# Adding the second gate block's halves on VectorE in the later feature-major chunks

## The chip, the core and the metric

The kernel runs on one core of a Trainium2 chip. The metric is the time of one execution on the device, in microseconds. A core has a matrix engine (TensorE, PE in the rows; its weight loads are listed apart as PEld), VectorE (DVE), ScalarE (ACT), GpSimd (POOL) and SyncE (SP), which issues most of the transfers. Every engine works through its own list of instructions in order, and semaphores tie the lists together.

## The reference

Two layers of a decoder on 256 tokens of width 1024, in float32: each layer has a gated feed-forward (FFN), a mixer and a second FFN, each followed by a layer norm. The change touches the FFN alone:

```python
def swiglu(x, w_in, w_out):
    gate, up = jnp.split(x @ w_in, 2, axis=-1)
    return (jax.nn.silu(gate) * up) @ w_out

x = layer_norm(ALPHA * x + 0.5 * swiglu(x, ffn1_w_in[l], ffn1_w_out[l]), ln_gain[l, 0], ln_bias[l, 0])
```

There are four FFNs, called F0, F1, F2 and F3; the mixers AB and C stand between F0 and F1 and between F2 and F3. The hidden width is 2816.

## The kernel before, in words

Float32 accuracy is made of products of rounded numbers: a weight w is split into w_hi, a rounded copy that ScalarE makes, and w_lo = w - w_hi, which VectorE makes; activations likewise. TensorE multiplies high by high and adds the two mixed products.

An FFN is cut into 11 chunks of 256 hidden features, numbered 0 to 10. For each chunk three units of weights come in from memory through a ring of three raw buffers (`raw`): two with the gate and up columns, and a product block with rows of `w_out`. Chunks 0, 1 and 10 are computed with tokens in the partitions. Chunks 2 to 9 are feature-major: features in the partitions, four blocks of 128 features in a chunk, the first two of the gate, the last two of the up half. A block (`up_block`) is one psum bank of 512 columns: 256 tokens with the high part of x beside the same 256 with its low part, both against w_hi, and the product with w_lo added to the first half. The two halves of 256 columns must still be added, for the gate before the Silu. All four blocks of a chunk use the same bank `G[0]`, so the next block's first matmul waits until ScalarE has copied the one before it out (`up_copy`, semaphore `up_copied`): gate blocks to `GATES` (which lies in `ffn_tok`), up blocks to `UPS`. Between the blocks TensorE has products of the chunk before (lines 2026), five or six matmul passes, to work on.

Who adds the halves: for the up blocks VectorE, both at once, line 1067 (`up_add`). For each gate block GpSimd issues a transfer from SBUF to SBUF that adds on its way, line 1717 (`add_gates`): 64 of them, two for each of the 32 feature-major chunks. ScalarE's Silu of both gate blocks (line 579) waits for both transfers. Then VectorE multiplies (`up_product`, line 1079), forms sums of hidden blocks (`hidden_sums`, lines 1043 to 1048; the down projection is a Strassen-like scheme with seven products) and sums of the next product block's weights (`weight_sums`, lines 1013 to 1019), which ScalarE rounds at line 515 ahead of the second gate block's copy.

The order on each engine is written out by hand. VectorE's list in one feature-major chunk: additions and sums as above, the rest of the hidden blocks (1053, 1059), the splits of the weight sums (1031) and of two gate and up units (995), and the split of the product block's rest (`split_plain_lo`, line 1001), which waits for ScalarE's cast of that block (line 509). Beside that VectorE makes rotary tables in chunks 4, 5 and 6 of F0, and prepares bounds of mixer C in chunk 4 of F1 and chunk 3 of F2 (`beside`). GpSimd's list holds the adding transfers, in F0 with loads of tables between them: a pool's weights behind chunk 4, constants behind chunk 5, and a norm's gain and bias behind chunk 6.

Of the kernel before, what the change touches and what calls it, by code (L numbers as in the profile page):

```python
# [17 lines left out]
ALU = mybir.AluOpType  # L18
# [9 lines left out]
SEQ = 256  # L28
# [7 lines left out]
N_PROD = NC - 2  # L36
N_COPY = 2
FIRST_FM = 2
N_FM = NC - 1 - FIRST_FM
STD_CHUNK = {0: 0, 1: 1, NC - 1: 2}  # L40
N_T = N_COPY + 2
# [34 lines left out]
def build(nc, x, positions, ln_gain, ln_bias, ffn1_w_in, ffn1_w_out, ffn2_w_in, ffn2_w_out, ab_w_in, ab_w_o,  # L76
          diff_lambda, diff_subln, pool_w, pool_scale, c_w_in, c_w_o, c_norm, hgrn_gamma, consts, out):
    with ExitStack() as ctx:
# [3 lines left out]
        def sem(name):  # L82
            return ctx.enter_context(nc.semaphore(name))
# [63 lines left out]
        sums_hi, sums_lo, sums_used = sem("sums_hi"), sem("sums_lo"), sem("sums_used")  # L147
        sums_half = sem("sums_half")
        up_done, up_copied = sem("up_done"), sem("up_copied")
        gate_added = [sem(f"gate_added{j}") for j in range(2)]  # L150
        up_added, x_added = sem("up_added"), [sem(f"x_added{i}") for i in range(4)]
        gate_silu, hid_product = sem("gate_silu"), sem("hid_product")
        early_used, late_hi, late_lo = sem("early_used"), sem("late_hi"), sem("late_lo")
# [55 lines left out]
        SILUS = {"F0": 0, "F1": 1, "F2": 2, "F3": 3}  # L209
# [19 lines left out]
        for m, name in enumerate(ORDER):  # L229
# [3 lines left out]
            for u, kind in enumerate(kinds):  # L233
# [20 lines left out]
                chunk = pairs - (kind == "B")  # L254
                if name in FFN and kind in "AB" and FIRST_FM <= chunk < NC - 1:
                    occupant[slot] = (up_done, 4 * (N_FM * SILUS[name] + chunk - FIRST_FM + 1), 0)
                elif kind in "AO":
# [94 lines left out]
        GATES = ffn_tok[:].rearrange("p a t f -> p (a t f)").rearrange("p (b f) -> p b f", b=2)  # L352
# [125 lines left out]
        def _(act):  # L478
# [88 lines left out]
            def up_copy(name, c, b):  # L567

                f = SILUS[name]
                act.wait_ge(up_done, 4 * (N_FM * f + c - FIRST_FM) + b + 1)  # L570
                if c > FIRST_FM:
                    act.wait_ge(hid_product, N_FM * f + c - FIRST_FM)
                nc.scalar.copy((UPS[name] if b // 2 else GATES)[:, b % 2], G[0]).then_inc(up_copied, 1)  # L573

            def gates_silu(name, c):

                for j in range(2):
                    act.wait_ge(gate_added[j], 16 * (N_FM * SILUS[name] + c - FIRST_FM + 1))
                nc.scalar.activation(GATES[:, :, 0:SEQ], GATES[:, :, 0:SEQ], ACT.Silu).then_inc(gate_silu, 1)

            def ffn(name, m):
# [42 lines left out]
                for c in range(FIRST_FM, NC - 1):  # L624
# [32 lines left out]
                    else:  # L657
# [7 lines left out]
                                     ).then_inc(copied_out, 1)  # L665
                act.wait_ge(hid_product, N_FM * (f + 1))
                act.wait_ge(sums_used, N_PROD * (f + 1))
# [313 lines left out]
        def _(dve):  # L981
# [8 lines left out]
            def split_lo(n):  # L990

                if n >= N_UNITS:
                    return
                dve.wait_ge(hi_ready, nth[n])
                nc.vector.tensor_tensor(w_lo[:, slot_of[n]], raw[:, n % RAW], w_hi[:, slot_of[n]].bitcast(F32),  # L995
                                        ALU.subtract).then_inc(lo_ready, 1)
# [37 lines left out]
            def hidden_sums(name, c):  # L1034
# [6 lines left out]
                else:  # L1041
                    dve.wait_ge(hid_product, N_FM * f + c - FIRST_FM + 1)
                nc.vector.tensor_tensor(s1, a21, a22, ALU.add).then_inc(hid_step1, 1)
# [12 lines left out]
            def hid_late_lo(name, c):  # L1056
# [2 lines left out]
                nc.vector.tensor_tensor(hT_lo_flat[:, LATE], hid_blocks[:, LATE_HID], hT_hi_flat[:, LATE].bitcast(F32),  # L1059
                                        ALU.subtract).then_inc(late_lo, 1)  # L1060

            def up_add(name, c):

                f = SILUS[name]
                ups = UPS[name]
                dve.wait_ge(up_copied, 4 * (N_FM * f + c - FIRST_FM + 1))
                nc.vector.tensor_tensor(ups[:, :, 0:SEQ], ups[:, :, 0:SEQ], ups[:, :, SEQ:], ALU.add
                                        ).then_inc(up_added, 1)
# [88 lines left out]
            def ffn_hidden(name, t, g, nth, hid):  # L1157

                dve.wait_ge(silu_ready, 2 * SILUS[name] * len(STD_CHUNK) + nth + 1)
                nc.vector.tensor_tensor(hid, g[:, FC:2 * FC], ffn_tok[:, 0, t], ALU.mult).then_inc(hid_ready, 1)  # L1160

            def ffn(name, m):
                s0, f = phases[name], SILUS[name]

                if m == 0:
                    ffn_hidden(name, 0, G[0], 0, ffn_tok[:, 1, 0])
                    weight_sums(name, s0 + 4, 0)
                    ffn_hidden(name, 1, G[1], 1, ffn_tok[:, 1, 1])
                    weight_sums(name, s0 + 4, 1)
                    split_lo(s0 + 3)  # L1170
                    split_plain_lo(s0 + 4)
                    hidden_sums(name, 0)
                    split_lo(s0 + 5)
                    hid_early_lo(name, 0)
                    ffn_hidden(name, 0, G[0], 2, ffn_tok[:, 0, 0])
                    ffn_hidden(name, 1, G[1], 3, ffn_tok[:, 0, 1])
                    hid_late_lo(name, 0)
                    split_sums_lo(name, s0 + 4, True)
                else:
                    xT_split(m, 0)  # L1180
                    norm(ORDER[m - 1], 1)
                    ffn_hidden(name, 0, G[0], 0, ffn_tok[:, 1, 0])
                    split_lo(s0 + 3)
                    xT_split(m, 1)
                    weight_sums(name, s0 + 4, 0)
                    weight_sums(name, s0 + 4, 1)
                    ffn_hidden(name, 0, G[1], 1, ffn_tok[:, 0, 0])
                    split_plain_lo(s0 + 4)
                    split_sums_lo(name, s0 + 4)
                    ffn_hidden(name, 1, G[0], 2, ffn_tok[:, 1, 1])  # L1190
                    if name == "F1" and BEFORE_C:
                        layer_c_tables()
                    hidden_sums(name, 0)
                    hid_early_lo(name, 0)
                    hid_late_lo(name, 0)
                    ffn_hidden(name, 1, G[1], 3, ffn_tok[:, 0, 1])
                    split_lo(s0 + 5)
                split_lo(s0 + 6)
                hidden_sums(name, 1)
                split_plain_lo(s0 + 7)  # L1200
                last = NC - 2
                for c in range(FIRST_FM, NC - 1):
                    n = s0 + 3 * c + 1
                    if c > FIRST_FM:
                        up_add(name, c - 1)
                        up_product(name, c - 1)
                        hidden_sums(name, c - 1)
                    weight_sums(name, n, 0)
                    weight_sums(name, n, 1)
                    if c == FIRST_FM + 1:  # L1210
                        split_lo(n + 1)
                        hid_early_lo(name, c - 1)
                    else:
                        hid_early_lo(name, c - 1)
                        split_lo(n + 1)
                    hid_late_lo(name, c - 1)
                    beside(name, c)
                    split_sums_lo(name, n)
                    split_lo(n + 2)
                    if c < last:  # L1220
                        split_plain_lo(n + 3)
                split_lo(n + 3)
                up_add(name, last)
                up_product(name, last)

                n, c = s0 + FFN_UNITS - 1, NC - 1
                dve.wait_ge(hidT_hi, NH * f + c)
                nc.vector.tensor_tensor(hT_lo[:, 0], hid_blocks[:, 0:512], hT_hi[:, 0].bitcast(F32), ALU.subtract
                                        ).then_inc(hidT_lo, 1)
                sums_out(name)  # L1230
                split_lo(n)
                ffn_hidden(name, 0, G[0], 4, ffn_tok[:, 1, 0])
                split_lo(n + 1)
                dve.wait_ge(x_added[0], 16 * (f + 1))
                dve.wait_ge(moved_out, 2 * f + 2)
                x0 = x_tok[:, 0].rearrange("p (h f) -> p h f", h=2)
                step(nc.vector.tensor_tensor(x0, x0, kept_both.unsqueeze(1).to_broadcast([P, 2, 512]), ALU.add))
                last_hidT(name, 0)
                split_lo(n + 2)
                norm_stats(name, 0)  # L1240
                norm_gain(name, 0, (0,))
                ffn_hidden(name, 1, G[1], 5, ffn_tok[:, 1, 1])
                norm_gain(name, 0, (1,))
                last_hidT(name, 1)
                norm_scale(name, 0)
                split_lo(n + 3)
# [443 lines left out]
        def _(pool):  # L1690
# [21 lines left out]

            def add_gates(name, chunks):
                for c in chunks:
                    for j in range(2):
                        pool.wait_ge(up_copied, 4 * (N_FM * SILUS[name] + c - FIRST_FM) + j + 1)
                        pool.dma_start(GATES[:, j, 0:SEQ], GATES[:, j, SEQ:], accum_op=ALU.add).then_inc(gate_added[j], 16)  # L1717

# [796 lines left out]
```

## Time and profile before

| | |
|---|---|
| Median of 3 runs | 965.91 us (965.4 to 967.02) |
| The profiled execution | 964.49 us, of which the profiled span is 962.8 us |
| Busy, TensorE / VectorE / ScalarE / GpSimd | 952.3 / 849.0 / 620.4 / 108.7 us |
| Granted TensorE clock | 0.998 of full |
| Moved by transfers | 197 MB, 205 GB/s in the mean |

The span is the time from the first to the last instruction of the profiled execution; the rest of its time lies around it. A row of the timeline gives start, duration, engine and line, what is written from what, and in brackets how long the engine was idle before it and what ended that. An engine that is busy for nearly all of the span need not be at its peak, since matmuls overlap and their ends are modelled.

### The profile page before, as it was taken

Reading aid. Unit: us, or ns where it says so; the run is one execution under the profiler, and the core shown is the slowest. Engines: PE = TensorE matmul, PEld = TensorE weight load, DVE = VectorE, ACT = ScalarE, POOL = GpSimd, SP = SyncE. Lnnn points to the kernel's source line nnn. Section 1 sums busy time; section 2 is a strip of 40 time slices with the busy share of each in tenths; the row PEclk is TensorE's granted clock in tenths of the full one; section 3 lists DMA queues with packets and bytes.
Section 4 is the critical chain, followed back from the end, with each engine's and each line's share of the span. In section 5 each row is a group of like instructions: output and inputs, shape, how many; then the busy total and the mean of one; then the engine's idle time right before and its main releaser. Section 6 shows DMA issues by size and latency. Waiting matters only on the chain.

```text
span 962.8 us, 13790 instructions
## 1 busy us (share of the span) xinstructions
PE 952.3 (99%) x4904; PEld 806.8 (84%) x4904; DVE 849.0 (88%) x1174; ACT 620.4 (64%) x727; POOL 108.7 (11%) x146
## 2 busy tenths in 40 slices
PE   9999999999999999999999999999999999999996
PEld 7888888888888888888888888888888888888885
DVE  5999998996898999889889989899898997999886
ACT  6776667436646667675576666549998546667660
POOL 0211111100210111110011101100100100111110
PEclk9999999999999999999999999999999999999999
DMA  9778877753656786876587777935243656786761
GB/s 306 240 228 234 280 235 223 232 178 129 223 180 205 217 244 193 236 227 206 173 237 235 239 231 232 271 124 184 89 131 115 235 192 190 215 242 194 237 162 55
DMA packets 140912, 197.31 MB, mean 205 GB/s; under 512 B 7280, under 2 KB 114336, under 8 KB 140720
## 3 DMA queue, kind: packets, MB, share of 16 engines
q1 hardware_dynamic: 126032, 173.56, 55.3%
q0 software_dynamic: 14256, 22.38, 11.1%
q8 instruction: 40, 0.66, 0.3%
q10 hardware_dynamic: 560, 0.52, 0.2%
q14 instruction: 24, 0.20, 0.1%
HBM read 182.79 MB, written 1.06 MB: 191 GB/s over the span
## 4 chain that ended last, share of the span: by engine, by line
PE 91%; DVE 5%; ACT 2%; issue 1%; DMA 1%; POOL 0%; DVEq 0%; SPq 0%; ACTq 0%
PE psum L2012 23%; PE psum L2026 15%; PE psum L2019 12%; PE psum L1821 12%; PE psum L1830 12%; PE psum L1825 12%; DVE w_lo L995 1%; PE psum L2402 1%; ACT w_hi L503 1%; PE psum L1814 1%; PE psum L2388 1%; DVE w_lo L1031 1%; DMA raw<-in_ffn_w_out 1%; DVE w_lo L1001 1%; PE psum L1996 1%
## 5 line engine op out<-in xcount | busy, mean ns | idle before, releaser
L995 DVE TENSOR_TENSOR w_lo<-raw,w_hi 128x2048 fp32r<-128x2048 f32 x125 | 285.1, 2284 | 20.9 <-ACT w_hi L503 20.8
L2012 PE MATMUL psum<-xT,w_hi 128*128 128x512 f32 x1024 | 254.2, 390 | 0.5
L503 ACT CAST w_hi<-raw 128x2048 fp32r<-128x2048 f32 x125 | 238.3, 1914 | 24.5 <-DMA raw<-in_ffn_w_in 15.0
L2012 PEld LDWEIGHTS psum<-xT,w_hi 128*128 128x128 f32 x1024 | 191.3, 188 | 44.8 <-ACT ffn_tok L573 3.2
L2019 PEld LDWEIGHTS psum<-xT,w_lo 128*128 128x128 f32 x1024 | 139.7, 190 | 10.0
L2019 PE MATMUL psum<-xT,w_lo 128*128 128x256 f32 x1024 | 142.8, 282 | 0.0
L1821 PE MATMUL psum<-w_hi,xT 128*128 128x512 f32 x447 | 128.7, 399 | 0.8 <-DVE arena L1538 0.4
L1830 PE MATMUL psum<-w_hi,xT 128*128 128x512 f32 x447 | 124.8, 390 | 0.2 <-DVE xT L1099 0.2
L1825 PE MATMUL psum<-w_lo,xT 128*128 128x512 f32 x447 | 124.7, 390 | 0.0
L1717 POOL DMA_DIRECT2D ffn_tok<-ffn_tok x64 | 55.0, 859 | 484.7 <-ACT ffn_tok L573 484.7
L1830 PEld LDWEIGHTS psum<-w_hi,xT 128*128 128x128 f32 x447 | 83.9, 188 | 18.3 <-DVE xT L1099 0.5
L1825 PEld LDWEIGHTS psum<-w_lo,xT 128*128 128x128 f32 x447 | 83.9, 188 | 17.7
L1821 PEld LDWEIGHTS psum<-w_hi,xT 128*128 128x128 f32 x447 | 80.8, 188 | 16.8 <-DVE ffn_tok L1160 0.8
L573 ACT COPY arena<-psum 128x512 f32<-128x512 f32 x64 | 37.6, 587 | 71.2 <-PE psum L2019 71.1
L1031 DVE TENSOR_TENSOR w_lo<-arena,w_hi 128x2048 fp32r<-128x2048 f32 x35 | 80.0, 2284 | 0.1
L1001 DVE TENSOR_TENSOR w_lo<-raw,w_hi 128x1536 fp32r<-128x1536 f32 x36 | 63.1, 1754 | 15.9 <-ACT w_hi L509 15.9
L573 ACT COPY ffn_tok<-psum 128x512 f32<-128x512 f32 x64 | 37.5, 586 | 59.3 <-PE psum L2019 45.1
L515 ACT CAST w_hi<-arena 128x2048 fp32r<-128x2048 f32 x36 | 68.9, 1915 | 10.5 <-DVE arena L1019 8.9
L2026 PE MATMUL psum<-w_hi,hT_hi 128*128 128x512 f32 x232 | 75.4, 395 | 0.0
L2026 PE MATMUL psum<-w_lo,hT_hi 128*128 128x512 f32 x232 | 75.1, 393 | 0.0
L2026 PE MATMUL psum<-w_hi,hT_lo 128*128 128x512 f32 x232 | 69.8, 393 | 0.0
L509 ACT CAST w_hi<-raw 128x1536 fp32r<-128x1536 f32 x36 | 53.5, 1485 | 14.5 <-PE psum L2026 7.9
(220 smaller groups left out, 1165.3 us busy)
## 6 DMA issues: line engine op xcount, KB each, us to landing
raw<-in_ffn_w_in SPq DMA_DIRECT2D x170, 512.0 KB, 5.2
raw<-in_ffn_w_out SPq DMA_DIRECT2D x88, 512.0 KB, 4.4
raw<-in_c_w_in SPq DMA_DIRECT2D x32, 512.0 KB, 4.7
ffn_tok<-ffn_tok POOLq DMA_DIRECT2D x64, 128.0 KB, 4.9
raw<-in_ab_w_in SPq DMA_DIRECT2D x16, 512.0 KB, 4.9
x_tok<-arena POOLq DMA_DIRECT2D x16, 256.0 KB, 7.3
raw<-in_ab_w_o SPq DMA_DIRECT2D x8, 512.0 KB, 4.2
raw<-in_c_w_o SPq DMA_DIRECT2D x8, 512.0 KB, 4.0
```

Source lines behind the costliest of these rows:

```text
L503: nc.scalar.copy(w_hi[:, slot_of[n]], raw[:, n % RAW]).then_inc(hi_ready, 1)
L515: nc.scalar.copy(w_hi[:, SUMS], SUM_PLACES[name].rearrange("p a f -> p (a f)")).then_inc(sums_hi, 1)
L573: nc.scalar.copy((UPS[name] if b // 2 else GATES)[:, b % 2], G[0]).then_inc(up_copied, 1)
L995: nc.vector.tensor_tensor(w_lo[:, slot_of[n]], raw[:, n % RAW], w_hi[:, slot_of[n]].bitcast(F32), ALU.subtract).then_inc(lo_ready, 1)
L1001: nc.vector.tensor_tensor(w_lo[:, PLAIN, 0:1536], raw[:, n % RAW, 512:], w_hi[:, PLAIN, 0:1536].bitcast(F32), ALU.subtract).then_inc(plain ...
L1031: nc.vector.tensor_tensor(w_lo[:, SUMS], SUM_PLACES[name].rearrange("p a f -> p (a f)"), w_hi[:, SUMS].bitcast(F32), ALU.subtract).then_in ...
L1821: nc.tensor.matmul(dst, a_hi, b_hi, start=first, stop=False)
L1825: ins = nc.tensor.matmul(dst, a_hi, b_lo, start=False, stop=final and last)
L1830: ins = nc.tensor.matmul(dst, a_lo, b_hi, start=False, stop=final and last)
L2012: nc.tensor.matmul(G[0], w_hi[:, slot_of[n + kh], at:at + P], xT_both[:, 4 * kh + k].rearrange("p a s -> p (a s)"), start=kh == k == 0, st ...
L2019: ins = nc.tensor.matmul(G[0][:, 0:SEQ], w_lo[:, slot_of[n + kh], at:at + P], xT_hi[:, 4 * kh + k], start=False, stop=kh == 1 and k == 3)
L2026: return nc.tensor.matmul(PROD[p], a[:, A_OF[p] * P:(A_OF[p] + 1) * P], w[:, slot, part * 512:(part + 1) * 512], start=start, stop=stop)
```

## The change

From the third feature-major chunk on (chunks 4 to 9 of each FFN, 24 of the 32) the halves of the second gate block are added by VectorE (`gate_sum`), placed between the split of the second gate and up unit and the split of the product block's rest; the transfer for it is not issued. The first gate block keeps its transfer, and chunks 2 and 3 keep both. The Silu waits for the new semaphore instead of the second transfer's.

```diff
+N_BY_DMA = 2
...
-        gate_added = [sem(f"gate_added{j}") for j in range(2)]
+        gate_added, gate_summed = [sem(f"gate_added{j}") for j in range(2)], sem("gate_summed")
...
             def gates_silu(name, c):
 
-                for j in range(2):
-                    act.wait_ge(gate_added[j], 16 * (N_FM * SILUS[name] + c - FIRST_FM + 1))
+                f, k = SILUS[name], c - FIRST_FM
+                act.wait_ge(gate_added[0], 16 * (N_FM * f + k + 1))
+                if k < N_BY_DMA:
+                    act.wait_ge(gate_added[1], 16 * (N_BY_DMA * f + k + 1))
+                else:
+                    act.wait_ge(gate_summed, (N_FM - N_BY_DMA) * f + k - N_BY_DMA + 1)
                 nc.scalar.activation(GATES[:, :, 0:SEQ], GATES[:, :, 0:SEQ], ACT.Silu).then_inc(gate_silu, 1)
...
+            def gate_sum(name, c):
+
+                dve.wait_ge(up_copied, 4 * (N_FM * SILUS[name] + c - FIRST_FM) + 2)
+                nc.vector.tensor_tensor(GATES[:, 1, 0:SEQ], GATES[:, 1, 0:SEQ], GATES[:, 1, SEQ:], ALU.add
+                                        ).then_inc(gate_summed, 1)
...
                     split_sums_lo(name, n)
                     split_lo(n + 2)
+                    if c >= FIRST_FM + N_BY_DMA:
+                        gate_sum(name, c)
                     if c < last:
                         split_plain_lo(n + 3)
...
                 for c in chunks:
-                    for j in range(2):
+                    for j in range(2 if c < FIRST_FM + N_BY_DMA else 1):
                         pool.wait_ge(up_copied, 4 * (N_FM * SILUS[name] + c - FIRST_FM) + j + 1)
                         pool.dma_start(GATES[:, j, 0:SEQ], GATES[:, j, SEQ:], accum_op=ALU.add).then_inc(gate_added[j], 16)
```

Line numbers of the changed kernel are higher by 5 on VectorE up to the new function and by 13 behind it. VectorE's list in chunk 4 of F0, from the split of the weight sums (1031) to the sum of the up halves (1067), before:

```order
L1282 TENSOR_SCALAR arena<-arena 128x64
L1283 TENSOR_SCALAR arena<-arena 128x64
L1031 TENSOR_TENSOR w_lo<-arena,w_hi 128x2048
L995 TENSOR_TENSOR w_lo<-raw,w_hi 128x2048
L1001 TENSOR_TENSOR w_lo<-raw,w_hi 128x1536
L1067 TENSOR_TENSOR arena<-arena 128x2x256
```

and in the changed kernel, where line 1070 is the new addition:

```order
L1295 TENSOR_SCALAR arena<-arena 128x64
L1296 TENSOR_SCALAR arena<-arena 128x64
L1036 TENSOR_TENSOR w_lo<-arena,w_hi 128x2048
L1000 TENSOR_TENSOR w_lo<-raw,w_hi 128x2048
L1070 TENSOR_TENSOR ffn_tok<-ffn_tok 128x256
L1006 TENSOR_TENSOR w_lo<-raw,w_hi 128x1536
L1078 TENSOR_TENSOR arena<-arena 128x2x256
```

One instruction has been put in ahead of the product block's rest; the rest of VectorE's order is the same. GpSimd's list in F0 before, from the transfers of chunks 2 to 4 on (ffn_tok is where the gates lie):

```order
L1717 DMA ffn_tok<-ffn_tok 128x256 x6
L1747 DMA arena<-in_pool_w 128x4x128
L1717 DMA ffn_tok<-ffn_tok 128x256 x2
L1749 DMA arena<-shape_constants 128x1536
L1717 DMA ffn_tok<-ffn_tok 128x256 x2
L1705 DMA ln_gb<-in_ln_gain 128x1024
L1705 DMA ln_gb<-in_ln_bias 128x1024
```

and in the changed kernel:

```order
L1730 DMA ffn_tok<-ffn_tok 128x256 x5
L1760 DMA arena<-in_pool_w 128x4x128
L1730 DMA ffn_tok<-ffn_tok 128x256
L1762 DMA arena<-shape_constants 128x1536
L1730 DMA ffn_tok<-ffn_tok 128x256
L1718 DMA ln_gb<-in_ln_gain 128x1024
L1718 DMA ln_gb<-in_ln_bias 128x1024
```

The loads of tables now stand behind the first transfer of chunks 4, 5 and 6, and no longer behind a second one.

## Rows read from the trace of the kernel before

**Rows 1.** The page: busy times of the engines, and the chain's shares.

```profile
PE 952.3 (99%) x4904; PEld 806.8 (84%) x4904; DVE 849.0 (88%) x1174; ACT 620.4 (64%) x727; POOL 108.7 (11%) x146
...
PE 91%; DVE 5%; ACT 2%; issue 1%; DMA 1%; POOL 0%; DVEq 0%; SPq 0%; ACTq 0%
```

**Rows 2.** F0, chunk 7: length, busy time by engine, clock, DMA share, GB/s.

```profile
114.91:130.84 15.93, 15.93 (x87) 13.77 (x86) 14.33 (x15) 11.04 (x12) 1.75 (x2) 1.00 0.86 268
```

**Rows 3.** Waits: who for whom; total us, times, longest.

```profile
DVE w_lo L1001 <- ACT w_hi L509: 15.9, 17, 1.1
...
PEld psum L2012 <- ACT ffn_tok L573: 3.2, 7, 0.6
...
ACT ffn_tok L579 <- DMA ffn_tok<-ffn_tok: 0.3, 1, 0.3
```

**Rows 4.** VectorE's timeline, F0, chunk 7: start, duration, instruction, idle before.

```profile
122.93 0.42 DVE L1059 TENSOR_TENSOR hT_lo<-arena,hT_hi 128x256 fp32r<-128x256 f32 x1
123.27 2.28 DVE L1031 TENSOR_TENSOR w_lo<-arena,w_hi 128x2048 fp32r<-128x2048 f32 x1
...
128.80 1.76 DVE L1001 TENSOR_TENSOR w_lo<-raw,w_hi 128x1536 fp32r<-128x1536 f32 x1 [1.05 <-ACT w_hi L509]
130.84 0.69 DVE L1067 TENSOR_TENSOR arena<-arena 128x512 f32<-128x512 f32 x1 [0.29 <-ACT arena L573]
```

**Rows 5.** VectorE in F1, chunk 4 and chunk 9.

```profile
343.48 1.76 DVE L1001 TENSOR_TENSOR w_lo<-raw,w_hi 128x1536 fp32r<-128x1536 f32 x1 [0.22 <-ACT w_hi L509]
...
423.99 2.29 DVE L995 TENSOR_TENSOR w_lo<-raw,w_hi 128x2048 fp32r<-128x2048 f32 x1 [1.63 <-ACT w_hi L503]
```

**Rows 6.** VectorE in F0: sums in chunks 5 and 6, end of 6.

```profile
88.11 0.69 DVE L1019 TENSOR_TENSOR arena<-raw,arena 128x512 f32<-128x512 f32 x1
...
103.77 0.69 DVE L1019 TENSOR_TENSOR arena<-raw,arena 128x512 f32<-128x512 f32 x1
...
114.91 0.69 DVE L1067 TENSOR_TENSOR arena<-arena 128x512 f32<-128x512 f32 x1 [0.29 <-ACT arena L573]
```

**Rows 7.** ScalarE in F0: copies and casts of chunks 5 to 7.

```profile
90.64 0.58 ACT L573 COPY ffn_tok<-psum 128x512 f32<-128x512 f32 x1
...
95.42 1.48 ACT L509 CAST w_hi<-raw 128x1536 fp32r<-128x1536 f32 x1 [0.40 <-PE psum L2026]
98.36 0.59 ACT L573 COPY arena<-psum 128x512 f32<-128x512 f32 x1 [1.46 <-PE psum L2019]
...
106.44 0.59 ACT L573 COPY ffn_tok<-psum 128x512 f32<-128x512 f32 x1
...
122.37 0.59 ACT L573 COPY ffn_tok<-psum 128x512 f32<-128x512 f32 x1 [0.35 <-PE psum L2019]
```

**Rows 8.** Weight loads in F0: third block of chunks 5 and 6.

```profile
91.28 0.19 PEld L2012 LDWEIGHTS psum<-xT,w_hi 128*128 128x128 f32 x1
...
107.17 0.19 PEld L2012 LDWEIGHTS psum<-xT,w_hi 128*128 128x128 f32 x1
```

**Rows 9.** All 64 adding transfers: time from issue to landing.

```profile
DMA to landing us min/median/max: 2.7/4.9/7.8
```

**Rows 10.** GpSimd's timeline in F0, chunk 5.

```profile
87.23 0.84 POOL L1717 DMA_DIRECT2D ffn_tok<-ffn_tok  x1 [9.95 <-ACT ffn_tok L573]
91.52 0.85 POOL L1717 DMA_DIRECT2D ffn_tok<-ffn_tok  x1 [3.44 <-ACT ffn_tok L573]
92.06 0.88 POOL L1749 DMA_DIRECT2D arena<-shape_constants  x1
```

**Rows 11.** Loads in F0: product block at 88.9, gate units at 91.9, 123.2.

```profile
L422 SPq DMA_DIRECT2D raw<-in_ffn_w_out x2: 346/346/346, 89.0 to 89.5; - x2
...
DMA to landing us min/median/max: 4.1/4.6/5.0
...
DMA to landing us min/median/max: 4.9/6.3/7.7
...
DMA to landing us min/median/max: 4.3/5.1/5.9
```

## The prediction

> **What bounds the kernel now.** Read the page's busy times first, then the chain: TensorE is busy 99% of the span and holds 91% of the chain that ended last [rows 1]. So time is won or lost only where TensorE waits. The stretch table says the same of one feature-major chunk, from one addition of the up halves to the next: 15.93 us, TensorE busy for all of it, VectorE for 14.33, the granted clock 1.00, the 2.4 GHz level [rows 2]. VectorE thus has 1.6 us of room in a chunk. Next the table of waits: the weight loads of the gate and up blocks waited 3.2 us in 7 places for a gate copy out of psum; VectorE waited 15.9 us in 17 places for ScalarE's cast of a product block; and ScalarE's Silu waited for the adding transfers once, for 0.3 us [rows 3]. That last row is all that the transfers cost visibly today.
>
> **What is removed.** Of 32 feature-major chunks 24 lose the transfer of the second gate block. The Silu waited 0.3 us for a transfer once [rows 3]. In its chunk the delay ended inside VectorE's own room, so I count this gain as nothing. The transfers' traffic (24 times 128 KB) lies beside weight loads that ScalarE reads without a wait in the steady chunks; I count that as nothing too.
>
> **What is added, and its price.** VectorE does 24 additions of 128x256 numbers, two operands and the result in SBUF. No row of before has just this one. The nearest is the 128x256 subtraction of line 1059: its own duration is 0.42 us, but the next instruction starts 0.34 us after it (122.93 to 123.27) [rows 4]. What a full VectorE loses is the distance of starts, so I take 0.34 and keep 0.42 as the upper end; the in-place addition of twice the size takes 0.69 [rows 4], so nothing dearer is near. The Trainium skill ("VectorE: DVE Perf Modes", section "The TRN2 errata — SBUF-src ops pay a fixed extra latency per instruction") puts an fp32 add at N plus 151 cycles of 0.96 GHz, which is 0.42 us as an estimate; by it the sum below would be 0.61 instead of 0.45. The trace agrees with that duration (0.42), but shows that the next start does not wait for all of it.
>
> **Where it lies.** The addition stands between the split of the second weight unit (line 995) and the split of the product block's rest (line 1001). In the steady chunk VectorE stands idle at this place, 1.05 us, until ScalarE's cast ends [rows 4]. It waits for a copy that ScalarE made before the cast that the split just ahead of it needs, so the new wait is met already, and nothing queues up behind it. The 17 idle places of line 1001 are all in changed chunks: fourteen of 1.05 us (two in F0, four each in F1, F2 and F3), one of 0.22 in chunk 4 of F1, and the chunks 4 of F2 and F3, which share the rest, 0.9. Where only 0.22 is free the rest, 0.12, goes into the 0.29 that VectorE waits one instruction later in a steady chunk [rows 4, 5]. In the four last chunks the idle place is before line 995, 1.63 us or more [rows 5]. That makes 21 of 24 additions that cost nothing; their cover is ScalarE's cast, and if that cover went each would cost up to 0.34.
>
> The other three are chunks 4, 5 and 6 of F0, where VectorE also makes the rotary tables and runs without a gap. There its delay goes on to TensorE this way: the weight sums (line 1019) come late, ScalarE's cast of them late, the copy of the second gate block behind it late, and the third block's weight load waits for that copy. From the sums' start to the copy are 2.53 us (88.11 to 90.64) in chunk 5, and the third block starts 0.64 after the copy does; in chunk 6 that distance is 0.73 [rows 6, 7, 8]. The shorter one I take for the least possible, so chunk 5 has no slack left. In chunk 6 the sums start at 103.77 and the copy could start at 106.30, but starts at 106.44 [rows 6, 7]. Slack 0.14, and 0.09 from the distance: 0.23. In chunk 7 the copy waits 0.35 for TensorE [rows 7], a slack of over 0.35.
> - Chunk 5: the addition of chunk 4 makes VectorE 0.34 late, and TensorE waits 0.34.
> - Chunk 6: two additions, 0.68, less the 0.34 that TensorE has shifted: 0.34 late, less 0.23 of slack: 0.11.
> - Chunk 7: 0.34 - 0.11 + 0.34 = 0.57 late, less the 0.29 idle before line 1067 [rows 6]: 0.28, within the slack: nothing. Then the 1.05 us of chunk 7 takes up the rest.
> Sum 0.45 us; with 0.42 an addition, 0.42 + 0.19 = 0.61. The lower end is 0: a delay that some gap takes up which I overlooked.
>
> **What moves with it.** GpSimd's queue is in order, and in F0 loads of tables stand behind the second transfer of a chunk. They now stand behind the first, 4.3 us earlier (87.23 for 91.52): the 128x1536 constants, 768 KB, leave at about 87.8 instead of 92.06 [rows 10], and the next norm's gain and bias behind chunk 6 as much earlier. They then run beside the load of a product block (issued at 88.98, landed by about 94.5 [rows 11]) instead of a gate and up unit. Before, the unit beside the constants landed 7.7 us after its issue, and one with a gate transfer alone beside it 5.9 us after [rows 11]: 1.8 us more. The product block is cast at 95.42 [rows 7], 0.9 us after it lands, so with 1.8 more the cast would be about 0.9 late. The copy behind that cast has an idle 1.46 before it [rows 7], which covers this. So zero. The far end: at the pace of the product block (twice 512 KB in 5.5 us) the constants' 768 KB are 4.2 us; less 0.9 and 1.46 this leaves 1.8 us of TensorE's time, and 5.5 us for the norm's two rows, as much again as a product block, with the same slacks 3.1: together 4.9. I take 0, near the measured 1.8 of delay, and keep 4.9 as the far end. The Trainium skill ("DMA: Bandwidth & Descriptors", section "SWDGE vs HWDGE vs iDMA") says that an engine takes turns between the queues of both kinds, so that the block would share its rate as long as the constants last: by that the delay would lie between the two ends, and no row here shows product loads beside constants. In F2 the same happens with two loads of a row of D numbers for all partitions, in chunks where VectorE and ScalarE have their steady room; I count nothing for it.
>
> **Sum.** 0.45 + 0 - 0 = 0.45 us: the profiled execution took 964.49 us (span 962.8 and 1.7 around it), so 964.9. The median of the runs, 965.91, lies 1.4 above that execution; the same 0.45 on it gives 966.4.
>
> **Rivals.**
> - *No change at all, or a trace of gain.* The transfers are late in executions that were not profiled: landing spreads from 2.7 to 7.8 us [rows 9], and the Silu was touched once. If the late ones cost TensorE 0.5 us a run, the change breaks even: 965.9. For it: the runs lie above the profiled one. Against: a late Silu costs only past VectorE's idle 0.29 and the copy's 0.35.
> - *A real gain*, over 1.9 us: the gate copies' whole 3.2 us of waits [rows 3] would have to go, 963. Against: the wait that I place lies in a chunk in which VectorE is full, and the changed chunks from 7 on show none.
> - *Slower by the moved tables.* In F0 the cast of a product block waits for its load, with it the fourth copy and the next chunk's first block. Price up to 4.9 on top of the 0.45: 971.3. It decides past 0.2% once the two loads together come more than 1.5 us beyond the slack. Against: the measured delay of 1.8.
> - *VectorE is the bound.* If ScalarE's cast came as much later as VectorE, the idle place would move along and all 24 additions count: 24 x 0.34 = 8.2, 974.1. Against: the cast waits for TensorE and not for VectorE in the steady chunk.
> - *The change doesn't do what it says*: the order shows the additions at their place, and none is folded away. No chance is kept for it.
>
> **How the numbers follow.** About 0.2%, 1.9 us, is what a measurement of this kernel can tell from no change. Forecast (its own range 965.9 to 966.7: an addition at 0 to 0.42, and some scatter) 0.62; break even or a little gain 0.20; real gain 0.05; moved tables 0.10, of which 0.03 stay within 0.2%; VectorE the bound 0.03. Faster 0.05, same 0.85, slower 0.10. The runs scatter from 965.4 to 967.02, so the range for 8 in 10 goes from 964.8 to 968.2; it takes in the first rival, part of the tables' delay, and leaves out the rest.
>
> **What would show it.** After: VectorE's 24 new additions of about 0.42 us, the idle time before line 1001's successor down from 15.9 to about 10 us, and no Silu waiting on VectorE. In F0 chunk 5 the third block's first weight load waits about 0.4 us for the gate copy, in chunk 6 about 0.1. The wait of ScalarE's cast of the gate unit for its load near 100 us (beside the constants) goes, and a cast of a product block waits for its load at about 96. Chunks 7 to 9 of every stage still take 15.93 us. Wrong would be: waits of TensorE in steady chunks, a Silu that waits for the sum, or a fourth copy late for the cast.

## The result, and the profile after

The changed kernel takes 968.58 us (median of 14 runs, 966.88 to 969.92), the kernel before beside it 966.42 us (14 runs, 965.17 to 968.15). The ratio is 1.0022, with an interval of 1.0014 to 1.0030: slower by 2.2 us, where 0.45 was forecast, and just past the range. The profiled execution took 968.88 us with a span of 967.1. That of the kernel before was one of its faster ones (964.49, its median 966.42), so the two traces lie 4.4 us apart and the medians 2.2.

The page of the kernel after, busy times and chain [rows 1]:

```profile
PE 953.2 (99%) x4904; PEld 806.7 (83%) x4904; DVE 856.5 (89%) x1198; ACT 619.8 (64%) x727; POOL 88.2 (9%) x122
...
PE 78%; DVE 13%; DMA 4%; ACT 3%; issue 2%; SPq 1%; POOL 0%; DVEq 0%; ACTq 0%
```

TensorE has the same work (953.2 for 952.3) and the span is 4.3 us longer. VectorE did 7.5 us more, GpSimd 20.5 us less. In the chain DMA has gone from 1 to 4%, though the change took transfers away. That names a suspect and no more: in kernel e2 below, which has lost nothing, it is 4% as well.

The steady chunk is unhurt. Stretches of the kernel after, from one addition of the up halves to the next, F0 chunk 6 and chunk 8; the columns are those of [rows 2]:

```profile
101.18:119.82 18.64, 16.95 (x90) 14.15 (x89) 15.27 (x23) 10.48 (x12) 1.98 (x3) 1.00 0.91 266
...
135.05:151.00 15.95, 15.95 (x87) 13.79 (x86) 14.66 (x16) 10.95 (x13) 0.87 (x1) 1.00 0.72 220
```

Chunk 8 lasts 15.95 us for 15.93 in chunk 7 before, with VectorE busy 14.66 for 14.33: the new 0.33 lies in room that it had. Chunk 6 lasts 18.64, and TensorE is idle for 1.7 of that, with the granted clock at 1.00. VectorE's timeline of the kernel after in chunk 8 [rows 4]:

```profile
147.85 0.42 DVE L1070 TENSOR_TENSOR ffn_tok<-ffn_tok 128x256 f32<-128x256 f32 x1
148.98 1.76 DVE L1006 TENSOR_TENSOR w_lo<-raw,w_hi 128x1536 fp32r<-128x1536 f32 x1 [0.71 <-ACT w_hi L510]
151.02 0.69 DVE L1078 TENSOR_TENSOR arena<-arena 128x512 f32<-128x512 f32 x1 [0.29 <-ACT arena L574]
```

The addition takes 0.42, the idle place behind it has shrunk from 1.05 to 0.71, by 0.34, and what follows waits as before. That is the cover that the prediction named, working as named.

The waits of the kernel after [rows 3]; PEld is a weight load, PE a matmul:

```profile
ACT w_hi L510 <- DMA raw<-in_ffn_w_out: 16.2, 11, 4.1
DVE w_lo L1006 <- ACT w_hi L510: 14.0, 14, 3.0
...
PEld psum L2025 <- ACT ffn_tok L574: 5.2, 10, 1.1
PEld psum L2025 <- ACT arena L574: 2.8, 2, 2.1
PE psum L2025 <- ACT arena L574: 1.9, 2, 1.7
PE psum L2025 <- ACT ffn_tok L574: 1.3, 3, 0.7
```

The Silu's wait is gone. The waits of up-block copies, 0.5 before, are now 2.8, 2.1 of that in one place, and ScalarE's cast of product blocks waits for loads 16.2 us in all (6.6 before), 4.1 of that in one place. To find the place, take the length of each chunk of F0 from the starts of its first block's weight loads (chunks 2 and 3 are alike in both kernels):

| F0 chunk | 2 and 3 | 4 | 5 | 6 | 7 | 8 |
|---|---|---|---|---|---|---|
| before | 32.33 | 16.17 | 15.93 | 15.93 | 15.93 | 15.93 |
| after | 33.38 | 16.11 | 15.97 | **18.09** | **16.54** | 15.93 |

From chunk 4 on that is 2.75 us, 2.16 of it in chunk 6 and 0.61 in chunk 7. The 1.05 of chunks 2 and 3, and 0.47 by which chunk 2 begins later, fall before anything is changed; the profiles of the eight experiments have 32.3 to 32.6 in chunks 2 and 3, so I count both as scatter of this one execution. After F0 the distance between the two traces hardly grows: F1 begins 4.61 us later, F3's last feature-major chunk 4.48.

The chain of the kernel after from 104 to 120 us: start, duration, what:

```profile
105.64 0.70 DVE arena L1024
...
107.07 9.56 DMA raw<-in_ffn_w_out
...
118.03 0.59 ACT arena L574
118.62 0.04 issue
118.66 1.43 PE psum L2025 x5
```

One half of chunk 6's product block is 9.56 us under way, the other 8.1; in the kernel before the same two took 4.5 and 3.7. What GpSimd issued just ahead of it, in the kernel after [rows 10]:

```profile
104.65 0.85 POOL L1730 DMA_DIRECT2D ffn_tok<-ffn_tok  x1 [14.56 <-ACT ffn_tok L574]
105.20 0.87 POOL L1718 DMA_DIRECT2D ln_gb<-in_ln_gain  x1
105.74 0.89 POOL L1718 DMA_DIRECT2D ln_gb<-in_ln_bias  x1
```

The norm's gain and bias, 512 KB each, now go out right before the product block's load. ScalarE's timeline of the kernel after shows what follows [rows 7]:

```profile
97.78 1.49 ACT L510 CAST w_hi<-raw 128x1536 fp32r<-128x1536 f32 x1 [1.27 <-DMA raw<-in_ffn_w_out]
99.84 0.59 ACT L574 COPY arena<-psum 128x512 f32<-128x512 f32 x1 [0.58 <-PE psum L2032]
...
116.65 1.47 ACT L510 CAST w_hi<-raw 128x1536 fp32r<-128x1536 f32 x1 [4.15 <-DMA raw<-in_ffn_w_out]
118.03 0.58 ACT L574 COPY arena<-psum 128x512 f32<-128x512 f32 x1
```

In chunk 5, beside the constants, the cast waits 1.27 us and the copy behind it still has 0.58 idle: covered. In chunk 6, beside the norm's rows, the cast waits 4.15 and the copy, with no idle left, is late. TensorE's weight loads in the kernel after, third blocks of chunks 5 and 6, then first and third of chunk 7 [rows 8]:

```profile
92.82 0.30 PEld L2025 LDWEIGHTS psum<-xT,w_hi 128*128 128x128 f32 x2 [0.18 <-ACT ffn_tok L574]
...
108.81 1.69 PEld L2025 LDWEIGHTS psum<-xT,w_hi 128*128 128x128 f32 x8 [0.20 <-ACT ffn_tok L574]
...
118.66 1.46 PEld L2025 LDWEIGHTS psum<-xT,w_hi 128*128 128x128 f32 x7 [2.13 <-ACT arena L574]
...
127.46 1.67 PEld L2025 LDWEIGHTS psum<-xT,w_hi 128*128 128x128 f32 x8 [0.85 <-ACT ffn_tok L574]
```

The forecast wait (0.18 and 0.20) is there and small; the 2.13 at the head of chunk 7 is the copy behind the late cast. The 0.85 after it is its echo: VectorE can split the late product block only behind the cast (118.16, for 1.76 us), so its additions and sums of chunk 7 come late, and with them the gate copy.

### The profile page after: what moved, and what is told of

The parts are those of the page before. It is cut to its first block, busy times and chain, and to the rows that moved or that the text cites. A ratio compares the mean times of both kernels' runs of the same rounds, so it can differ in the third digit from the quotient of the medians.

```text
span 967.1 us, 13790 instructions
## 1 busy us (share of the span) xinstructions
PE 953.2 (99%) x4904; PEld 806.7 (83%) x4904; DVE 856.5 (89%) x1198; ACT 619.8 (64%) x727; POOL 88.2 (9%) x122
## 4 chain that ended last, share of the span: by engine, by line
PE 78%; DVE 13%; DMA 4%; ACT 3%; issue 2%; SPq 1%; POOL 0%; DVEq 0%; ACTq 0%
PE psum L2025 19%; PE psum L2039 12%; PE psum L1834 11%; PE psum L1838 10%; PE psum L1843 10%; PE psum L2032 10%; DVE w_lo L1000 4%; DMA raw<-in_ffn_w_out 3%; DVE w_lo L1036 2%; ACT w_hi L504 1%; DVE w_lo L1006 1%; DMA raw<-in_ffn_w_in 1%; PE psum L2415 1%; PE psum L1827 1%; PE psum L2401 1%
## 5 line engine op out<-in xcount | busy, mean ns | idle before, releaser
L1730 POOL DMA_DIRECT2D ffn_tok<-ffn_tok x40 | 34.4, 860 | 492.3 <-ACT ffn_tok L574 492.3
L510 ACT CAST w_hi<-raw 128x1536 fp32r<-128x1536 f32 x36 | 53.4, 1484 | 22.6 <-DMA raw<-in_ffn_w_out 16.2
```

## The experiments

The theory (T or B in the expectations): the cost is the moved tables, above all the norm's rows ahead of chunk 6's product block. Its rivals: the additions on a VectorE without a gap in F0 (V), and of the moved tables the constants behind chunk 5 rather than the norm. Each kernel was timed in 5 rounds against the kernel before. The chunk lengths are taken from one profile each, as above:

| Kernel | us | beside | ratio [interval] | chunks 4, 5, 6, 7 of F0 | product block of chunk 6, us to landing |
|---|---|---|---|---|---|
| after | 968.58 | 966.42 | 1.0022 [1.0014, 1.0030] | 16.11 15.97 18.09 16.54 | 8.1 and 9.6 |
| e1_hold_tables | 966.10 | 966.35 | 0.9997 [0.9988, 1.0006] | 16.09 16.08 16.41 15.93 | 3.6 and 4.7 |
| e2_hold_norm | 966.12 | 966.35 | 1.0001 [0.9991, 1.0011] | 16.17 15.97 15.98 15.93 | 3.7 and 4.4 |
| e3_tables_alone | 967.75 | 966.35 | 1.0016 [1.0007, 1.0024] | 16.17 15.93 16.20 16.56 | 6.7 and 7.9 |
| e4_f0_transfers | 966.76 | 966.35 | 1.0006 [0.9997, 1.0014] | 16.15 15.95 16.77 15.93 | 4.0 and 5.4 |
| e5_half_norm | 967.55 | 966.32 | 1.0008 [1.0000, 1.0017] | 16.18 15.97 16.28 16.57 | 6.9 and 7.7 |
| e6_norm_behind | 966.65 | 966.32 | 1.0004 [0.9995, 1.0013] | 16.19 15.97 15.98 16.25 | 3.8 and 7.1 |
| e7_rope_later | 966.18 | 966.32 | 1.0003 [0.9991, 1.0016] | 16.17 15.93 15.93 15.93 | 3.7 and 5.3 |
| e8_before_rope_later | 966.00 | 966.32 | 0.9998 [0.9988, 1.0008] | 16.37 15.93 15.93 15.93 | 3.7 and 4.4 |

**Tables held in their old place (e1).** GpSimd waits for the second gate copy, as it did when it had a transfer for it; the additions stay.

```diff
+                    if c >= FIRST_FM + N_BY_DMA:
+                        pool.wait_ge(up_copied, 4 * (N_FM * SILUS[name] + c - FIRST_FM) + 2)
```

> The changed kernel, with GpSimd waiting for the second gate block's copy before it goes on, so that the tables of F0 and F2 are issued at the time they had before; all 24 additions stay on VectorE. Theory T (the loads of tables, issued 4.3 us earlier, take their rate from the product block's load): the time comes back to 0.2 to 0.8 us above the kernel before (ratio about 1.0005), chunks 6 and 7 of F0 lose the 2.1 and 0.6 us that they gained, and the cast of the product block in chunk 6 no longer waits 4.1 us for its load. Rival V (the additions on a full VectorE): stays 2.2 us above (ratio 1.0022).

The loss is gone; that the median lies 0.25 below the kernel before and not 0.2 to 0.8 above it, the interval doesn't separate. Chunk 6 is 0.48 longer than before: the constants now stand beside a gate and up unit again, whose cast waited 1.9 us for its load in this profile. A row of TensorE's weight loads in this kernel, second block of chunk 6:

```profile
104.58 1.68 PEld L2027 LDWEIGHTS psum<-xT,w_hi 128*128 128x128 f32 x8 [0.61 <-ACT ffn_tok L574]
```

**Only the norm's rows held (e2).** The same wait, behind chunk 6 of F0 alone; pool weights and constants stay early.

```diff
+                    if name == "F0" and c == 6:
+                        pool.wait_ge(up_copied, 4 * (N_FM * SILUS[name] + c - FIRST_FM) + 2)
```

> The changed kernel, in which GpSimd waits for the second gate copy in chunk 6 of F0 alone, so that only the norm's gain and bias (two loads of 512 KB) go back to their old time; the pool's weights and the constants stay early. T: nearly all of the loss is the norm's rows, so 0.3 to 1.0 us above the kernel before; the constants still make the cast of chunk 5 wait about 1.3 us, inside its slack of 1.46. If the constants mattered as much: 1.2 to 2 above. V: 2.2 above.

One wait in one place takes the whole loss away, so neither the additions nor the constants carry it by themselves: both rivals fall. The product block's load in this kernel (times of its two issues, and to landing), and ScalarE's timeline at the place of the late cast:

```profile
L423 SPq DMA_DIRECT2D raw<-in_ffn_w_out x2: 345/345/345, 105.7 to 106.3; - x2
...
DMA to landing us min/median/max: 3.7/4.0/4.4
```

```profile
112.09 1.49 ACT L510 CAST w_hi<-raw 128x1536 fp32r<-128x1536 f32 x1 [0.40 <-PE psum L2041]
115.03 0.59 ACT L574 COPY arena<-psum 128x512 f32<-128x512 f32 x1 [1.45 <-PE psum L2034]
```

The cast waits for TensorE as it did before, 1.4 us after the load landed (106.26 + 4.40 = 110.66), and the copy has 1.45 idle before it. The slack is thus 1.43 + 1.45 = 2.88, and a delay of 9.56 - 4.40 = 5.16 us leaves 2.28: the wait that the trace of the kernel after shows is 2.13. The 4.40 is one execution's: the table has 4.4 to 5.4 for this half where no rows stand ahead, so a delay read from one profile is good to about 1 us.

**The tables early, without the additions (e3).** In chunks 4 to 6 of F0 the second gate block is added by nobody; this part of the work is left out.

```diff
+            return "none" if name == "F0" and c in (4, 5, 6) else "sum"
...
-                    if c >= FIRST_FM + N_BY_DMA:
+                    if gate_kind(name, c) == "sum":
                         gate_sum(name, c)
```

> The changed kernel with the tables early as in the change, but in chunks 4, 5 and 6 of F0 the second gate block's halves are not added at all (left out of the computation), so VectorE's list in these chunks is that of before. T: 1.5 to 2.3 us above the kernel before, with the first block of F0's chunk 7 waiting about 2 us. V: no slower than before, within 0.3 us.

The loss is there with VectorE relieved. ScalarE's cast and TensorE's two waits in this kernel:

```profile
114.06 1.48 ACT L520 CAST w_hi<-raw 128x1536 fp32r<-128x1536 f32 x1 [2.33 <-DMA raw<-in_ffn_w_out]
```

```profile
116.08 1.67 PEld L2038 LDWEIGHTS psum<-xT,w_hi 128*128 128x128 f32 x8 [0.32 <-ACT arena L584]
124.88 1.68 PEld L2038 LDWEIGHTS psum<-xT,w_hi 128*128 128x128 f32 x8 [0.88 <-ACT ffn_tok L584]
```

The first wait is smaller than in the kernel after, and than the 2 us expected (0.32 for 2.13), the echo the same. The block's second half landed after 7.94 us, 3.54 late, though the same 1,024 KB stand ahead of it. The rows were issued 1.05 us ahead of the block here (104.49 and 105.54) and 1.32 in the kernel after. The intervals of the two kernels overlap, so whether the additions make the collision worse is not settled.

**The change in F1 to F3 alone (e4).** F0 keeps all transfers (the edit is to the function `gate_kind` of the kernel above, which here never returns "none").

```diff
-            if c < FIRST_FM + N_BY_DMA or False:
+            if c < FIRST_FM + N_BY_DMA or name == "F0":
                 return "transfer"
```

> The change in F1, F2 and F3 alone; F0 keeps both transfers and its order on GpSimd. T: within 0.4 us of the kernel before. V with a price in every chunk: three quarters of 2.2, about 1.6 above; V with the price in F0 alone: also 0, so this run tells whether the additions outside F0 cost anything.

The interval holds no change, and chunks 4, 5 and 7 of F0 are as before; chunk 6 shows once more the constants beside a unit (a wait of 0.96 at its second block). So the loss needs F0's change.

**Half of the norm's rows early (e5).** The other halves, 512 KB of 1,024, go out behind chunk 8.

```diff
...
-            load_gb(0)
+            load_gb_half(0)
+            add_gates("F0", (7, 8))
+            load_gb_half(1)
...
```

> The changed kernel with half of each of the norm's two rows (512 KB in all instead of 1,024) early behind chunk 6's first gate copy, the other halves behind chunk 8's. Theory B (the product block's load is late by the bytes of the tables that are moved ahead of it, about 5 us for 1,024 KB): about 2.5 us late here instead of 5.1, so the cast in chunk 6 waits some 1.5 to 2 us instead of 4.15, TensorE's first block of chunk 7 waits under 0.3, and the time is 0.2 to 0.8 above the kernel before. Rival F (a price for each load that stands ahead, whatever its size): the cast waits 4 us again, time 2.2 above.

The product block's landing in this kernel:

```profile
L423 SPq DMA_DIRECT2D raw<-in_ffn_w_out x2: 346/346/346, 105.7 to 106.2; - x2
...
DMA to landing us min/median/max: 6.9/7.3/7.7
```

Half the bytes delay it by 7.75 - 4.40 = 3.35 us, 0.5 past the slack, and chunk 6 is 0.35 longer than in steady state, with the echo of 0.64 in chunk 7. The delay is less than in the kernel after, but more than the 2.5 of theory B, and about the 3.54 that the whole 1,024 KB gave in e3: that the delay goes with the bytes is not shown, and rival F is not excluded. The time, 1.2 above the runs beside it, is some tenths above what I had expected, and by the interval no more than a trend.

**The norm's rows issued together with the product block (e6).** GpSimd waits for the sums that also release the block's load.

```diff
+            pool.wait_ge(w_sums, nth[phases["F0"] + 3 * 6 + 1])
             load_gb(0)
```

> The changed kernel with the norm's two loads, whole, issued when the weight sums of chunk 6 are done: that same event lets the product block's load go, so both start together, about 1 to 2 us later than in the change and 2 us before their old time. Theory B with an order (what is ahead in the transfer engines goes first): the block lands 2 to 3 us late instead of 5.1, the cast waits 1 to 2 us, time 0.2 to 0.8 above the kernel before. If rates are shared evenly whatever the order: the block still 4 to 5 us late, time 1.5 to 2.2 above.

GpSimd's timeline and the landing of the product block, issued at 105.47 and 106.02, in this kernel:

```profile
105.58 0.55 POOL L1718 DMA_DIRECT2D ln_gb<-in_ln_gain  x1 [1.12 <-DVE arena L1024]
106.12 0.58 POOL L1718 DMA_DIRECT2D ln_gb<-in_ln_bias  x1
```

```profile
DMA to landing us min/median/max: 3.8/5.5/7.1
```

The first half of the block, issued 0.11 ahead of the first row, lands as if alone (3.8); the second, issued between the two rows, is 2.7 late. For the copy that is inside the slack: chunk 6 keeps its 15.98. VectorE's split is late all the same, and the echo makes chunk 7 0.33 longer; the time, 0.33 above the runs beside it, is in the range expected.

Moved in the 3.5 us from about the issue of the block's second half on, in the kernel after (107.0 to 110.5), which has no row of SyncE's queue q1; q0 is GpSimd's (packets, MB, share of the engines; a packet counts where it starts):

```profile
q0 software_dynamic: 202, 0.76, 101.4%
```

and in e3 (106.0 to 109.5):

```profile
q0 software_dynamic: 192, 0.60, 61.7%
q1 hardware_dynamic: 88, 0.36, 31.6%
```

In the kernel after the block stood still while the rows moved. In e5, with half of them, it did too (0.42 MB and nothing); in e6 both queues moved (0.42 and 0.52), and in e3 as well, though there the block was issued behind the rows. So the block came latest where it was issued 1.32 us behind all the rows, and least late where it was issued with them; what decides between standing still and sharing stays open.

**A better kernel?** The rotary tables moved to chunks 7 to 9 of F0 and the bounds of C to chunk 4 of F2, where VectorE has room: on top of the held norm (e7), and in the kernel before (e8).

```diff
-                if name == BEFORE_AB and c in (4, 5, 6):
-                    rope_tables(c - 4)
+                if name == BEFORE_AB and c in (7, 8, 9):
+                    rope_tables(c - 7)
...
```

> A candidate: the change with the norm's rows held to their old place (as the kernel with ratio 1.0001), and the rotary tables of F0 made in chunks 7, 8, 9 instead of 4, 5, 6, the bounds of mixer C in chunk 4 of F2 instead of 3. In the trace of before the chunks 4 and 5 of F0 wait 0.4 us and chunk 4 of F2 0.5 for a late VectorE; all theories: these waits go, 0.5 to 1.0 us below the kernel before (ratio about 0.9993), if the additions cost nothing in steady chunks; no gain if VectorE's new work in chunks 7 to 9 is late there.

> The kernel before with the same two moves of VectorE's side work alone, all gate blocks added by transfers. If the moves bring the gain and the change none: the same time as the candidate with the change, 0.5 to 1.0 us below the kernel before. If the change itself is worth something once its tables are out of the way: this one is slower than that candidate.

In the profile of e7 chunks 5 to 8 all take 15.93, so the last trace of the additions is gone. Of the waits that were to go, the one in chunk 4 of F2 is gone in both (15.98 and 15.97 for 16.35); the one in chunk 4 of F0 is still there (16.17 and 16.37 for 16.17). No time beats the kernel before: both intervals hold 1. The one run of e7 at 971.78 is not explained. No version here is measurably better than the kernel before.

## Why the prediction was wrong

- *TensorE is the bound, and 21 of 24 additions cost nothing*: right. The idle place gave up 0.34 of 1.05, the additions take 0.42, the start behind one comes 0.34 later, and the steady chunks of all four FFNs stay at 15.93 to 15.97, but for two of F2: chunk 4 takes 16.47 for 16.35 and chunk 7 16.01. The idle time before the product block's split, forecast at about 10 us, is 14.0 in the kernel after, 3.0 of it behind the late cast, and 10.4 with the norm held.
- *The delay through chunks 4 to 6 of F0, 0.45*: right in its path, too large. With the norm held, chunks 4, 5 and 6 are together 0.09 us longer than before (0, 0.04, 0.05). Two things were missed. First, VectorE lost only part of an addition in chunk 4: from the weight sums of chunk 4 to those of chunk 5 its list took 15.97 for 15.88, and 15.98 for 15.66 in the next chunk; the cause is below. Second, a weight load's wait does not reach TensorE whole. With the norm held (e2) the third blocks' loads of chunks 4, 5 and 6 wait 0.36, 0.16 and 0.19 us, 0.71 together, and the three chunks are 0.33 longer than three of 15.93: about 0.13 of each wait is absorbed, and the rest passes on. The table of waits does not show this. Its rows of weight loads and of matmuls for a gate copy in e2:

```profile
PEld psum L2027 <- ACT ffn_tok L574: 3.5, 10, 0.6
...
PE psum L2027 <- ACT ffn_tok L574: 0.2, 1, 0.2
```

  Ten late loads, one late matmul, and that one in F2: the chunks' lengths tell the price, not these rows. I had passed a load's delay on to TensorE one for one.
- *The constants beside a product block cost nothing*: right. The block lands 6.7 us after its issue, 1.6 later than before (5.0) and near the 1.8 that I took; the cast waits 1.27, and the 1.46 of slack covers it. The far end had charged 4.2 for these 768 KB.
- *"I take 0, near the measured 1.8 of delay, and keep 4.9 as the far end"*: this is the step that failed, for the norm's two rows. I priced them by the one collision of before, constants issued behind a unit's load. In the changed kernel the rows are issued 1.3 us ahead of the product block, and the delay is 5.16: nearly the 5.5 of the far end, which charged the whole of their bytes. It is past the 2.88 of slack (I had 0.9 + 1.46), and TensorE's weight loads wait 2.13. So nearly all of the 2.2 us comes from the term that I set to 0, and not from the 0.45. The far end's 3.1 us for them stands beside 2.77 measured in chunks 6 and 7 of the profile, echo included, and 2.2 in the medians. That the far end came so near is in part luck: by the same rule the constants should have been 4.2 late and were 1.6, and e3 has 3.54 for the same rows. The mechanism of the rival "Slower by the moved tables" was the right one, at a chance of 0.10. Before, the same rows stood behind the unit's load (issued at 107.58, the rows at 107.86 and 108.41), and no product block waited behind them; that order could be read ahead of the run, and it should have kept the norm's rows from being priced at nothing. The Trainium skill ("DMA: Bandwidth & Descriptors", section "SWDGE vs HWDGE vs iDMA") says that an engine takes turns between the queues of both kinds. The traces of e3 and e6, where both queues moved, agree; in the kernel after and in e5 the block's queue moved nothing for 3.5 us, and taking turns alone does not give that.
- *The removed transfers gain nothing*: right, as far as the interval goes. With the norm held, 24 transfers fewer leave the time where it was (1.0001 [0.9991, 1.0011]).

## What to carry to other kernels

An instruction taken from a queue that runs in order moves all that stands behind it: list what moves up, and for each moved transfer ask which load it now stands ahead of. Don't price it by a collision in which it was issued second, and don't count on its bytes alone: here 768 KB ahead cost a load 1.6 us, 512 KB 3.4, and 1,024 KB once 3.5 and once 5.2. If the far end would be felt, hold the transfer back by a wait. And read a wait of a weight load as an upper bound for TensorE's.

## What the runs showed of the hardware

VectorE's small scalings of the rotary tables are slower while GpSimd writes out transfers. VectorE in chunk 4 of F0 before, and GpSimd's timeline of the same stretch:

```profile
76.31 0.63 DVE L1281 TENSOR_SCALAR arena<-arena,pos_f 128x32 f32<-128x32 f32 x2
76.97 0.33 DVE L1282 TENSOR_SCALAR arena<-arena 128x64 f32<-128x64 f32 x1
77.34 0.19 DVE L1283 TENSOR_SCALAR arena<-arena 128x64 f32<-128x64 f32 x1
```

```profile
75.64 0.85 POOL L1717 DMA_DIRECT2D ffn_tok<-ffn_tok  x1 [3.73 <-ACT ffn_tok L573]
76.18 1.11 POOL L1747 DMA_DIRECT2D arena<-in_pool_w  x1
```

The same two in the kernel after:

```profile
77.76 0.52 DVE L1294 TENSOR_SCALAR arena<-arena,pos_f 128x32 f32<-128x32 f32 x2
78.31 0.20 DVE L1295 TENSOR_SCALAR arena<-arena 128x64 f32<-128x64 f32 x1
78.55 0.20 DVE L1296 TENSOR_SCALAR arena<-arena 128x64 f32<-128x64 f32 x1
```

```profile
72.58 0.85 POOL L1730 DMA_DIRECT2D ffn_tok<-ffn_tok  x1 [10.94 <-ACT ffn_tok L574]
73.12 1.10 POOL L1760 DMA_DIRECT2D arena<-in_pool_w  x1
```

With GpSimd at work until 77.29 the third of these rows starts 1.03 us after the first; with GpSimd idle, 0.79. Where F0 keeps its transfers (e4) the first two last 0.63 and 0.33 again, with the tables early and no additions (e3) 0.52 and 0.19. These 0.24 us paid for most of the 0.34 of chunk 4's addition. The Trainium skill ("SBUF — State Buffer", section "SBUF: two separate sides") has VectorE, in some kinds of its instructions, and GpSimd share a pair of ports from which whichever starts first locks out the other. The rows agree in direction, and no run here separates that lock from another cause.
